# A loop on TensorE over experts 8 to 29, six weight slots for them, expert 1's one-hot columns earlier, and one row of the fourth expert's down weights in a place of its own

## The reference

```python
def hierarchical_moe(h, w_rg, b_rg, w_re, b_re, w_gu, w_dn):
    g_logits = xt @ w_rg + b_rg                 # 4 groups, the best one is taken
    e_in = e_logits[arange(t), grp]             # its 8 experts
    top_v, top_i = lax.top_k(e_in, 2)           # two of them for each token
    gate = p_grp * softmax(top_v)
    ...
    def expert_block(args):                     # for each of 32 experts
        gg, uu = split(xblk @ w_gu[e], 2)       # w_gu[e]: 1024 x 1024
        return (silu(gg) * uu) @ w_dn[e]        # w_dn[e]: 512 x 1024
    ...
out = rmsnorm(x + hierarchical_moe(rmsnorm(x), ...))
```

## Time and profile before

| | us |
|---|---|
| median of three runs | 970.23 |
| lowest and highest of them | 968.17, 970.36 |
| the profiled execution, its own time | 968.7 |
| its span in the trace | 966.9 |

### The profile page before, as it was taken

One profiled execution on the slowest core, in us unless ns is written; L12 is line 12 of the kernel. 1 busy time (PEld: TensorE's weight loads), 2 busy tenths in 40 slices (PEclk: granted clock), 3 DMA queues, 4 the chain that ended last, 5 costly groups with the idle time before them and its releaser, 6 DMA issues.

```text
span 966.9 us, 18379 instructions
## 1 busy us (share of the span) xinstructions
PE 819.8 (85%) x8064; PEld 652.9 (68%) x8064; DVE 338.8 (35%) x864; ACT 190.1 (20%) x354; POOL 324.4 (34%) x169
## 2 busy tenths in 40 slices
PE   8999999999999999999999996676757657566575
PEld 7999988889999999999887653333333333333232
DVE  2688323647263434343214352212112112121112
ACT  2521138731231000102012111011110111100102
POOL 5876630038998879996300000000000000000000
PEclk9999999999999999999999999879888898998988
DMA  9844535443465444447697999999999999999994
GB/s 312 252 175 176 180 126 163 142 154 109 175 218 174 142 161 147 167 171 270 222 427 309 413 426 426 427 428 427 426 427 427 426 428 426 427 427 426 428 425 190
DMA packets 62405, 285.32 MB, mean 295 GB/s; under 512 B 6692, under 2 KB 11640, under 8 KB 50168
## 3 DMA queue, kind: packets, MB, share of 16 engines
q1 hardware_dynamic: 58056, 280.84, 73.0%
q10 hardware_dynamic: 4272, 3.32, 1.2%
HBM read 283.08 MB, written 1.06 MB: 294 GB/s over the span
## 4 chain that ended last, share of the span: by engine, by line
PE 59%; DMA 25%; SPq 7%; DVE 2%; another core or an unknown queue 2%; ACT 2%; POOL 1%; issue 1%; ACTq 0%; DVEq 0%; POOLq 0%
PE bank L1678 31%; DMA blk<-in_w_down_dram 9%; PE bank L1576 7%; SPq L418 6%; DMA params<-in_w_down_dram 5%; DMA ring<-in_w_down_dram 5%; DMA ring<-in_w_gate_up_dram 5%; PE bank L1673 5%; PE bank L1950 5%; PE bank L1976 3%; PE bank L1644 1%; SPq L453 1%; PE bank L1916 1%; PE bank L1832 1%
## 5 line engine op out<-in xcount | busy, mean ns | idle before, releaser
L1678 PE MATMUL bank<-blk,ring 128*128 128x128 f32 x1840 | 213.4, 275 | 0.4 <-POOL blk L546 0.4
L1678 PEld LDWEIGHTS bank<-blk,ring 128*128 128x128 f32 x1840 | 209.3, 192 | 1.9 <-issue 1.8
L1950 PE MATMUL bank<-ring,cbm 128*32 128x256 f32 x1088 | 77.6, 433 | 40.7 <-DMA ring<-in_w_gate_up_dram 40.7
L1421 DVE TENSOR_TENSOR cbm<-bank,gq 128x256 f32<-128x256 f32 x31 | 13.2, 424 | 249.9 <-PE bank L1916 249.9
L1950 PEld LDWEIGHTS bank<-ring,cbm 128*32 128x32 f32 x1088 | 39.4, 122 | 73.1 <-issue 51.0
L1576 PE MATMUL bank<-blk,ring 128*128 128x256 f32 x384 | 85.4, 381 | 0.8 <-DVE blk L1343 0.8
L1950 PE MATMUL bank<-blk,cbm 128*32 128x256 f32 x768 | 55.8, 439 | 34.6 <-DMA blk<-in_w_gate_up_dram 34.5
L1576 PEld LDWEIGHTS bank<-blk,ring 128*128 128x128 f32 x384 | 72.2, 190 | 11.6 <-DVE blk L1343 1.2
L510 POOL TENSOR_TENSOR ring<-ring 128x1024 f32<-128x1024 f32 x20 | 47.3, 2364 | 97.1 <-DVE dec L1141 75.6
L1678 PE MATMUL bank<-ring 128*128 128x128 f32 x608 | 71.0, 275 | 0.0
L1678 PEld LDWEIGHTS bank<-ring 128*128 128x128 f32 x608 | 69.4, 192 | 0.0
(11 more groups left out here) (345 smaller groups left out, 1081.2 us busy)
## 6 DMA issues: line engine op xcount, KB each, us to landing
ring<-in_w_gate_up_dram SPq DMA_DIRECT2D x34, 2048.0 KB, 50.0
blk<-in_w_gate_up_dram SPq DMA_DIRECT2D x24, 2048.0 KB, 49.7
ring<-in_w_in_dram SPq DMA_DIRECT2D x19, 2048.0 KB, 7.9
ring<-in_w_down_dram SPq DMA_DIRECT2D x18, 2048.0 KB, 49.7
blk<-in_w_down_dram SPq DMA_DIRECT2D x10, 2048.0 KB, 50.2
params<-in_w_gate_up_dram SPq DMA_DIRECT2D x6, 2048.0 KB, 50.6
ring<-in_w_kv_dram SPq DMA_DIRECT2D x4, 2048.0 KB, 8.1
params<-in_w_down_dram SPq DMA_DIRECT2D x3, 2048.0 KB, 49.8
```

The lines of the kernel that those rows point to most:

```text
L1421: v.tensor_tensor(xeN, gu_bank(p)[:, T:2 * T], gq[:, :], ALU.mult).then_inc(sem["xn3_ready"], 1)
L1678: last = mm(out_[:, f], wt[:, k, f * P:(f + 1) * P], xt[:, k, :], start=k == 0, stop=k == 3)
L1950: last = mm(gu_bank(p)[c * WIN:(c + 1) * WIN, 0:2 * SEG], xe[:, xin, 4 * j + k, :], w[:, k, :, c, :], start=4 * j + k == 0, stop=4 * j + k ...
```

## The change

- **PE.** Experts 0 to 7, 30 and 31 stay written out. Experts 8 to 29 become a loop of eleven rounds with two experts each (`STEADY = 8`). Semaphore values in it are worked out from the loop's register.
- **Slots.** Parts 0 to 23 keep their slots. From part 24 on only six slots are used, `STEADY_TURNS = (3, 4, 5, 0, 1, 2)`, so that two experts fill them exactly and every round names the same ones. `home(k)` gives the slot of a part and `tenants` the parts that had it before; SP waits for the last of them.
- **One row early.** Part 11 is the down weights of expert 3 (`DIVIDED`). Its slot, `params`, comes free with expert 0's first half. The first of its four rows of 128 x 1024 now goes to a tile of its own, `early` (512 KB), as soon as `rk0` is done; the other three (1.5 MB) follow into `params` where the whole part went before. PE waits for `early_filled` ahead of expert 3's down matmuls.
- **Where the room is from.** `early` also holds, up to then, what were the tiles `onesm`, `mask`, `wr` and `dtw`. The small tiles `c8`, `csN`, `sm`, `br`, `dcol`, `bnst`, `bnag` are put together in `odd`, which later serves as the scratch row `ovs`.
- **DVE.** `one_hot` for expert 1 stands ahead of the steps that make the token weights; it needs ranks only. The first loop of two rounds is written out, so that this can be.

```diff
-    SPARE = TURNS[-PARTS:]
+    SPARE = (8, 9, 10)
+    STEADY = 8
+    STEADY_TURNS = (3, 4, 5, 0, 1, 2)
+    DIVIDED = RING // PARTS
+    def home(k):
+        return TURNS[k % RING] if k < PARTS * STEADY else STEADY_TURNS[k % len(STEADY_TURNS)]
+    def tenants(s, k):
+        return [m for m in range(k) if home(m) == s]
...
+        early = sb("early", [P, D])
+        onesm, mask = early[:, 0:P], early[:, P:4 * P]
...
-            for k in range(RING, PARTS * NE - 1):
-                sp.wait_ge(sem[USED[(k - RING) % PARTS]], (k - RING) // PARTS + 1)
-                part(k // PARTS, k % PARTS, TURNS[k % RING])
...
+            down = w_down[0, DIVIDED].rearrange("(p k) n -> p k n", p=P)
+            sp.wait_ge(sem["unit_done"], U["rk0"] + 1)
+            sp.dma_start(early[:, :], down[:, 0, :]).then_inc(sem["early_filled"], 16)
+            for k in range(RING, PARTS * NE):
+                m = tenants(home(k), k)[-1]
+                sp.wait_ge(sem[USED[m % PARTS]], m // PARTS + 1)
+                if k == RING:
+                    sp.dma_start(slot(TURNS[0])[:, D:].rearrange("p (k n) -> p k n", n=D), down[:, 1:, :]
+                                 ).then_inc(filled[TURNS[0]], 16)
+                elif k < PARTS * NE - 1:
+                    part(k // PARTS, k % PARTS, home(k))
...
+            one_hot(1, 1, lambda t: pw[:, t, 1:2])
             link(v.reduce_sum(rv("es"), rt2("ee"), AX.X))
...
-            with dve.Fori(0, 2) as i:
-                for p in range(2):
-                    e = i * 2 + (p + 1)
-                    window(e, e, 1, 1 - p)
-                    hidden(i * 2 + p, p)
+            choose(1, 1, 1)
+            place(1, 1, 1)
+            collect(1, 1)
+            hidden(0, 0)
+            window(2, 2, 1, 0)
+            hidden(1, 1)
+            for p in range(2):
+                window(3 + p, 3 + p, 1, 1 - p)
+                hidden(2 + p, p)
...
+                    if divided and k == 0:
+                        pe.wait_ge(sem["early_filled"], 16)
+                    wk = early if divided and k == 0 else w[:, k, :]
...
-            for e in range(NE):
+            for e in range(STEADY):
+                expert(e)
+            with pe.Fori(0, (NE - STEADY) // 2 - 1) as i:
+                for p in range(2):
+                    k = PARTS * (STEADY + p)
+                    ffn(i * 2 + (STEADY + p), p, [home(k + j) for j in range(PARTS)], p,
+                        lambda j: (i + fills(k + j)) * 16, True)
+            for e in range(NE - 2, NE):
                 expert(e)
```

More of the change, by code:

```diff
@@ L135, in encoder_kernel, with fills @@
     assert NSLAB % PRE == 0
-    SPARE = TURNS[-PARTS:]
[L137 to L141, removed]
+    SPARE = (8, 9, 10)
+    STEADY = 8
+    STEADY_TURNS = (3, 4, 5, 0, 1, 2)
+    DIVIDED = RING // PARTS
+    assert RING % PARTS == PARTS - 1
+    def home(k):
+        return TURNS[k % RING] if k < PARTS * STEADY else STEADY_TURNS[k % len(STEADY_TURNS)]
+    def tenants(s, k):
+        return [m for m in range(k) if home(m) == s]
+    def fills(k, s=None):
+        s = home(k) if s is None else s
         before = PREFILLS - (s == 0) if s < PRE else 0
-        return before + k // RING + 1
+        return before + len(tenants(s, k + 1))
+    assert STEADY % 2 == 0 and len(STEADY_TURNS) == 2 * PARTS
     ctx = ExitStack()
@@ L214, in encoder_kernel @@
         ones = sb("ones", [P, P])
-        onesm = sb("onesm", [P, P])
-        mask = sb("mask", [P, 3 * P])
+        early = sb("early", [P, D])
+        onesm, mask = early[:, 0:P], early[:, P:4 * P]
+        wr = early[:, 4 * P:4 * P + KD * (NG + NE)].rearrange("p (k n) -> p k n", k=KD)
+        dtw = early[:, 4 * P + KD * (NG + NE):].rearrange("p (a n) -> p a n", a=7)
+        assert 4 * P + KD * (NG + NE) + 7 * NT * HEADS == D
+        odd = sb("odd", [P, 224])
         COUNT = T + WIN
@@ L231, in encoder_kernel @@
                              .rearrange("p (g n) -> p g n", g=SGU_G) for i in range(3))
-        dcol = sb("dcol", [P, KD])
         stat = sb("stat", [P, 32])
-        c8 = sb("c8", [P, 6, KD])
-        dtw = sb("dtw", [P, 7, NT * HEADS])
-        csN = sb("csN", [P, NT, HEADS])
+        places = [(6, KD), (NT, HEADS), (4, XA_HEADS * NT), (1, NG + NE), (1, KD), (NT * 2, 6), (NT, 2)]
+        at = [sum(a * n for a, n in places[:i]) for i in range(len(places) + 1)]
+        assert at[-1] <= 7 * 32
+        c8, csN, sm, br, dcol, bnst, bnag = (odd[:, at[i]:at[i + 1]].rearrange("p (a n) -> p a n", a=a)
+                                             for i, (a, n) in enumerate(places))
+        br, dcol = br[:, 0, :], dcol[:, 0, :]
+        bnst = bnst.rearrange("p (t h) n -> p t h n", t=NT)
         csT = prow[:, :, :].rearrange("p a n -> p (a n)")
@@ L288, in encoder_kernel @@
         assert NOV * NE + NE * NMORE <= RT
-        ovs = mask[0:1, P:3 * P]
+        ovs = odd[0:1, :]
         ov_i = sb("ov_i", [1, 2 * NOV + 2], I32)
@@ L323, in encoder_kernel @@
             product mid_copied weights_ready combos_ready gate_ready c_rms x1_rms
-            wr_ready x2sq_ready x2fold x2sum_ready x2_rinv gexp_in gexp_done texp_in texp_done assign_ready
+            wr_ready early_filled x2sq_ready x2fold x2sum_ready x2_rinv gexp_in gexp_done texp_in texp_done assign_ready
              ov_ready half_done gu_done gathered dn_done xn3_ready xe_ready chosen_ready hot_ready placed_ready
@@ L479, in _ @@
             g.memset(ident[:], 0.0)
-            g.memset(onesm[:], 1.0 / D)
-            g.memset(mask[:], 1.0)
+            g.memset(onesm, 1.0 / D)
+            g.memset(mask, 1.0)
             g.memset(sguwT, 0.0)
@@ L1931, in spread_gfin, with ffn @@
                        start=True, stop=True).then_inc(sem["gfin_spread"], 1)
-            def ffn(n, p, slots, xin, arrived, behind, rows=False, opening=False):
+            def ffn(n, p, slots, xin, arrived, behind, rows=False, opening=False, divided=False):
                 if not behind:
@@ L1974, in ffn @@
                         pe.wait_ge(row_filled[k], 16)
+                    if divided and k == 0:
+                        pe.wait_ge(sem["early_filled"], 16)
+                    wk = early if divided and k == 0 else w[:, k, :]
                     for q in range(NQ):
                         last = mm(down_bank[q * WIN:(q + 1) * WIN, 0:COLS], hmT[:, k * WIN:(k + 1) * WIN],
-                                  w[:, k, q * COLS:(q + 1) * COLS], start=k == 0, stop=k == NF - 1)
+                                  wk[:, q * COLS:(q + 1) * COLS], start=k == 0, stop=k == NF - 1)
                 last.then_inc(sem["dn_done"], 1)
@@ L1984, in expert @@
             def expert(e):
-                slots = [TURNS[(PARTS * e + j) % RING] for j in range(PARTS)]
-                ffn(e, e % 2, slots, e % 2, lambda j: 16 * fills(PARTS * e + j), True, e == NE - 1, e == 0)
-            for e in range(NE):
+                slots = [home(PARTS * e + j) for j in range(PARTS)]
+                ffn(e, e % 2, slots, e % 2, lambda j: 16 * fills(PARTS * e + j), True, e == NE - 1, e == 0, e == DIVIDED)
+            for e in range(STEADY):
[6 more added lines that the diff above has]
+            for e in range(NE - 2, NE):
                 expert(e)
@@ L1996, in _ @@
                     ffn(o + NE, 0, SPARE, 1,
-                        lambda j: (o + ((PREFILLS - (SPARE[j] == 0) if SPARE[j] < PRE else 0) + SPARE_FILLS + 1)) * 16, False)
+                        lambda j: (o + (fills(PARTS * NE - 1, SPARE[j]) + 1)) * 16, False)
                     scatter(o + NE, 0)
```

9 lines of the change are left out of this document (1 added, 8 removed).

## The result

| | before | changed |
|---|---|---|
| median of five runs, us | 969.07 | 963.98 |
| lowest and highest, us | 968.17, 970.36 | 963.45, 965.08 |
| span of the profiled execution, us | 966.9 | 962.1 |

The ratio is 0.9946, with a 95% interval of 0.9935 to 0.9957. The same kernel run again on another chip, beside the last experiments, gave 0.9958 (0.9944 to 0.9971).

A forecast was written before the change was run, and what follows sets the result against it. After a front that PE bounds, the weights' stream was taken to set the end. Early row -1.23, columns -0.3, slots 0 and loop 0 gave -1.5 us: 968.7 us against the median of 970.23, range 966.0 to 971.5.

The forecast's parts named there:

- What bounds the kernel: PE full to 580 us, then the weights' stream at 425 to 428 GB/s; only its start, holes and rate count.
- Early row and columns: Window 529 to 545 us: row fills part of a hole, -1.23 us; earlier one-hot columns advance part 12, -0.3 us.
- the hole: Stream window from 529 to 533 us at 225 GB/s, a loss of 1.89 us; forecast to move 350 GB/s or more.
- Six slots: Six slots instead of eleven from part 24 on: queue can't run empty because of them, rate holds; cost 0.
- The 19 us to spare: With six slots: 22.6 us of transfers left when a slot frees, less some 3.3 us until the stream is back.
- the seam: From 520 to 580 us, where PE works through parts that came in ahead and catches up with the stream.
- The loop: PE's loop: added instructions hidden in waits; code fetches between -0.84 us (stays on chip) and +0.42 us (three per round); taken as 0.
- rival B: PE's loop branch fetches code when needed, some 4 us a packet, three in series: slower, about 992 us; chance 0.05.
- Rival A: All at once: early row closes its hole, second window stays full, code stays on chip; about 966.9 us; chance 0.12.
- C: Rival: a shorter queue slows the stream by 5% over the loop's 320 us, costing 16 us; about 986 us; chance 0.03.
- D: Rival: the early row gains nothing, its transfer running later or the end hanging on something else; 970.2 us; chance 0.10.
- The signs of being wrong: A stream slice below 420 GB/s after 560 us, PE idle above 10 us at the loop's start, or time before 520 us moving.

## Why the prediction was wrong

**What bounds the kernel: right.** The weights' stream sets the end, and only its start, its holes and its rate count. What I left out is that it is sixteen streams, and that the last of them is the end. The rows were there: the last slice of rows 1 moves 190 GB/s, and I read it as the output and the tail.

**Early row and columns: right in the sum, and as to why.** 1.5 us forecast, 1.3 and 1.4 measured, each within about a microsecond. The single shares are not confirmed. I gave the row 1.23 us and the columns 0.3; alone the row gave 0.2 and the columns 0.9, both within their noise nothing. That the sum came out so near is partly luck: the hole reached 298 GB/s and not 350. The sentence that without the columns the early row would open a small hole at part 12 had the mechanism, and only its size was too small: 1.0 us.

**Six slots: right.** No cost that can be measured (1.0004). The rows on the queue between 490 and 510 us decided it. The 19 us to spare hold for the steady part only; at the seam they don't, as the loop from expert 6 on showed.

**The loop: here the step failed.** "What remains is the code itself": I saw that each expert's code costs a packet of 16 KB, and priced the packets by their bytes against the whole stream, 22 packets = 0.36 MB = 0.84 us, with an end at -0.84 and +0.42, and took 0. The loop gave 3.4 to 4 us. Two things were wrong with it. A packet costs its engine 1.54 us; of the stream's own 16 KB packets an engine does one in 16 x 16.4 KB / 427 = 0.61 us. And this cost lies on one engine, not on sixteen: 22 packets on 8 engines are nearly 3 on each, and 3 x 1.54 = 4.6 us on the slowest, of which the runs show 3.4 to 4. Half of the price was in the prediction: rival B worked out 1.1 us for a packet of q8, and the sum didn't use it. Rival A had the right direction, code that stays on the chip, and ended at 966.9 for the same reason.

**Taking the middle between the ends.** Between "stays" and "is fetched three times" I took 0. The runs say that a body of two experts stays: 2 packets in 300 us. An estimate of its size from rows 9: 21 packets for 300 / 14.7 = 20.4 experts, so 2.06 packets of 16 KB for two, some 33 KB.

**The rivals.** B, a wait for code at the branch, did not come at the loop's branch. It came elsewhere: at the jump over the overflow rounds, 2.2 to 2.7 us, in two kernels, by the reading above because of where its target lay. The rule named there (the Trainium skill, "Runtime: NRT & Kernel Launch", section "Instruction fetch mechanics"), that a taken branch out of the pages at hand waits for a fetch, agrees with these two jumps. As to the loop's own branch, the same section of the Trainium skill speaks of a window of two pages of 16 KiB, and in another sentence of 128 KiB for PE. A body of some 33 KB that isn't fetched again agrees with the second figure; it is too near to the first to speak for or against it. C, a slower stream with a shorter queue, is out: 427 GB/s with the slots alone. D, an early row that gains nothing, fits the row alone, with another mechanism: the gain was given back one part later.

**The signs of being wrong.** None of the three that I had named shows. From 553 us to the last but one slice the stream stays at 426 GB/s or more, PE's longest wait at the loop's start is 3.0 us, and the time before 520 us moved by 0.3 us (part 9 is issued at 518.06). They watched for losses; the last slice, where the gain came, I had not looked at.

## What to carry to other kernels

This stream was spread over all DMA engines and ended with its slowest engine. In such a stream, in the last microseconds, read the rate as a count of engines that still run. Price everything that takes turns with it (code packets above all) on one engine and not by bytes, and see whether that engine has time to spare. In a stretch that DMA bounds, a loop is worth more than its instructions, and it can be checked in one row: the packets of the instruction queue. And two edits that feed the same hole have to be priced together, for one alone may only move it.

## What the runs showed of the hardware

- A 16 KB packet of PE's code held up one DMA engine by 1.54 us, an 8 KB packet of SP's code by 0.71 us. By the landings PE's packets went round 8 of the 16 engines; SP's all held up one.
- 23 packets of SP's code, 0.19 MB in all, made a kernel of 964 us 13.4 us slower, 12 of them 5.4 us, 3 of them nothing.
- A loop body on PE, by estimate some 33 KB, was not fetched again from round to round (2 packets in 300 us instead of 21). Its eleven branches cost nothing that can be seen in the time; PE waits for weights in every expert anyway.
- PE's jump over the code for overflow rounds cost 2.2 and 2.7 us in two kernels, while q8 fetched a packet; with the code moved by about 4 KB, both waits were gone. In the other kernels they never came.
- With six slots for parts of 2 MB, and nothing else changed, the stream moved as much (427 GB/s) as with eleven (427 GB/s), with landings, by the median, 27.3 us after the issue instead of 50.0.
